# The inputs loaded ahead of the modulation slabs and squared as they lie, and the first norm and first two panels taken by rows 0 to 3, then 4 to 7

## What is computed

```python
def rmsnorm(x, w):
    xf = x.astype(jnp.float32)
    y = xf * lax.rsqrt(jnp.mean(xf * xf, axis=-1, keepdims=True) + EPS)
    return (y * w.astype(jnp.float32)).astype(x.dtype)
...
    silu_c = jax.nn.silu(c)
    silu_cc = jax.nn.silu(c_ctx)[None]
    for i in range(DEPTH):
        mod_l = jnp.split((silu_c @ ada_w[i] + ada_b[i])[:, None], 6, axis=-1)
        mod_c = jnp.split((silu_cc @ ada_w[i] + ada_b[i])[:, None], 6, axis=-1)
        h_lat = rmsnorm(x_lat, norm_w[i, 0]) * (1 + sc_l) + sh_l
        h_ctx = rmsnorm(x_ctx, norm_w[i, 0]) * (1 + sc_c) + sh_c
        ...
        # hgrn2_mixer: q, zf, zb, v, g = split(h @ w_in, ...)
```

## Time and profile before

| | |
|---|---|
| median of three runs | 2220.25 us (2220.06, 2220.25, 2223.41) |
| the profiled execution, its own time | 2224.3 us |
| its span in the profile | 2222.4 us |
| mean granted TensorE clock | 0.977 of full speed |
| PE busy over the span | 2111.2 us, 95% |
| DVE, ACT, POOL busy | 1091.4, 824.9, 49.1 us |
| read from and written to DRAM | 189.47 MB and 13.63 MB |

### The profile page before, as it was taken

One profiled execution on the slowest core, in us unless ns is written; L12 is line 12 of the kernel. 1 busy time (PEld: TensorE's weight loads), 2 busy tenths in 40 slices (PEclk: granted clock), 3 DMA queues, 4 the chain that ended last, 5 costly groups with the idle time before them and its releaser, 6 DMA issues.

```text
span 2222.4 us, 33823 instructions
## 1 busy us (share of the span) xinstructions
PE 2111.2 (95%) x13397; PEld 1882.9 (85%) x13412; DVE 1091.4 (49%) x1607; ACT 824.9 (37%) x1278; POOL 49.1 (2%) x79
## 2 busy tenths in 40 slices
PE   5899999998989999999999889999998898999998
PEld 3799989998889999999999877787875687888887
DVE  4755555567352222222223686777777544333333
ACT  2543343345132221112221543838383425532222
POOL 1000000000000000000000100000001000000000
PEclk8999999999989999999999999999999999999999
DMA  7322222223314332233322211121215132333331
GB/s 273 128 77 77 86 86 75 69 86 100 119 48 142 113 98 66 73 114 114 118 69 58 83 54 45 48 85 47 85 47 203 56 92 78 100 101 89 95 111 68
DMA packets 297512, 204.42 MB, mean 92 GB/s; under 512 B 5012, under 2 KB 289037, under 8 KB 295629
## 3 DMA queue, kind: packets, MB, share of 16 engines
q1 hardware_dynamic: 293965, 180.03, 26.7%
q0 software_dynamic: 3456, 23.09, 2.8%
HBM read 189.47 MB, written 13.63 MB: 91 GB/s over the span
## 4 chain that ended last, share of the span: by engine, by line
PE 79%; DVE 10%; ACT 6%; issue 3%; DMA 1%; SPq 0%; ACTq 0%; DVEq 0%; POOL 0%
PE G L309 66%; PE G L415 2%; PE S L765 1%; PE S L1492 1%; DVE acc L1523 1%; ACT whi L292 1%; ACT e L1367 1%; DVE hlo L646 1%; PE S L736 1%; PE S L1488 1%; DVE wlo L296 1%; DVE hn L638 1%; PE S L1688 1%; DVE cum L985 1%; PE G L421 1%
## 5 line engine op out<-in xcount | busy, mean ns | idle before, releaser
L309 PE MATMUL G<-hhi,whi 128*128 128x384 f32 (+2 forms) x2336 | 726.8, 369 | 31.7 <-DVE hlo L646 20.5
L309 PE MATMUL G<-hhi,wlo 128*128 128x384 f32 (+2 forms) x2336 | 680.8, 349 | 0.0
L309 PE MATMUL G<-hlo,whi 128*128 128x384 f32 (+2 forms) x2336 | 680.5, 349 | 0.0
L296 DVE TENSOR_TENSOR wlo<-raw,whi 128x1024 fp32r<-128x1024 f32 (+1 forms) x225 | 288.4, 1282 | 779.5 <-ACT whi L292 779.2
L292 ACT ACTIVATE whi<-raw 128x1024 fp32r<-128x1024 f32 (+1 forms) x225 | 248.7, 1106 | 941.0 <-PE G L309 470.5
L309 PEld LDWEIGHTS G<-hhi,whi 128*128 128x128 f32 x2336 | 422.7, 191 | 98.0 <-issue 35.1
L309 PEld LDWEIGHTS G<-hhi,wlo 128*128 128x128 f32 x2336 | 432.9, 190 | 20.4
L309 PEld LDWEIGHTS G<-hlo,whi 128*128 128x128 f32 x2336 | 432.8, 190 | 17.9
L309 PE MATMUL G<-mhi,whi 128*128 128x384 f32 (+2 forms) x550 | 165.6, 346 | 0.0
L309 PE MATMUL G<-mlo,whi 128*128 128x384 f32 (+2 forms) x550 | 165.2, 345 | 0.0
L309 PE MATMUL G<-mhi,wlo 128*128 128x384 f32 (+2 forms) x550 | 165.2, 345 | 0.0
(11 more groups left out here) (283 smaller groups left out, 2098.3 us busy)
## 6 DMA issues: line engine op xcount, KB each, us to landing
raw<-in_ffn_w_in_dram SPq DMA_DIRECT2D x88, 512.0 KB, 3.7
raw<-in_ffn_w_out_dram SPq DMA_DIRECT2D x32, 704.0 KB, 4.5
raw<-in_ssm_w_in_dram SPq DMA_DIRECT2D x41, 512.0 KB, 3.8
raw<-in_hg_w_in_dram SPq DMA_DIRECT2D x40, 512.0 KB, 3.8
adaw<-in_ada_w_dram SPq DMA_DIRECT2D x20, 1024.0 KB, 5.8
adaf<-in_ada_w_dram SPq DMA_DIRECT2D x20, 1024.0 KB, 4.9
ada<-in_ada_w_dram SPq DMA_DIRECT2D x4, 2048.0 KB, 13.3
raw<-in_ssm_w_out_dram SPq DMA_DIRECT2D x16, 512.0 KB, 3.9
```

The costliest lines, as they stand in the source:

```text
L296: dve.tensor_tensor(wlo[pn.slot][:, 0:kt, :], raw[pn.slot][:, 0:kt, :], f32(whi[pn.slot][:, 0:kt, :]), ALU.subtract).then_inc(s["lo"], 1)
L309: ins = pe.matmul(G[:, tl.slot, g0:g0 + n], w[pn.slot][:, k, :], r[:, k_base + k, t0:t0 + n], start=(first and k == 0 and i == 0), stop=(l ...
```

## The change

It has four parts. (1) SP: the six inputs are issued ahead of all slabs, each on its own semaphore; then slab 2 and slab 0, the panels 0 and 1, slab 3 and slab 1 (`SLABS`). The first two slabs get tiles of their own, laid over `hhi` and `hlo`, so no slab waits for a tile. Slab 2 and 0 hold the scale and shift of rows 0 to 3, slab 3 and 1 those of rows 4 to 7. (2) The squares: ACT squares each input block as it lies, with the tokens on the partitions (`sqx`, 128 x 1024), and DVE sums a block with one `tensor_reduce` into `xsum`; the sums over channels on PE are gone, and all six blocks get one mean, one power on POOL, and one spread. (3) The transposes come ahead of the slabs on PE, and the first two slabs' `strips` and `turned` behind them. (4) `norm_place` makes the first norm go by rows 0 to 3 (half 0, then half 1), then rows 4 to 7; `product_first` replaces `product_pair` in the same order, with the other two slabs' `strips` after units 2 and 4 and their `turned` after units 5 and 7; ACT copies their rows to `arow` ahead of units 5 and 7 (`first_rows`), DVE adds them into `mods` ahead of units 7 and 8 and makes the second half of `afac` (`first_mods`). The `adaw` rows come with the last unit. The copy of `x0` to DRAM now waits for unit 9 of the norm as well, and the five small operations on `lbt` and `lb` stand behind the norm on DVE.

```diff
@@ squares, norm @@
+        def norm_place(N, v):
+            return (v // KT, v % KT) if N else (v % KT // 4, v // KT * 4 + v % 4)
@@ slabs @@
+        SLABS = (2, 0, 3, 1)
+        ada, arow = (m["adahi"], m["adalo"], m["ada0"], m["ada1"]), (m["arow0"], m["arow1"])
+        def slab_strips(pe, i):
+            pe.wait_ge(s[f"slab{i}"], 16)
+            strips(pe, [(S[:, i % 2, :], ada[i])]).then_inc(s["ada"], 1)
+        def product_first(pe, pn):
+            product_begin(pe, pn, pn)
+            for u in range(2 * KT + LAG):
+                if u < 2 * KT:
+                    e, k = norm_place(0, u)
+                    pe.wait_ge(s["hlo"], u + 1)
+                    ins = product_block(pe, pn, pn, m["hhi"], m["hlo"], k, KT, SEGS, half=e, apart=False)
+                if u == 2 * KT - 1:
+                    product_end(pe, pn, ins, rows=0)
+                if u == LAG:
+                    product_begin(pe, pn + 1, pn + 1)
+                if u >= LAG:
+                    e, k = norm_place(0, u - LAG)
+                    ins = product_block(pe, pn + 1, pn + 1, m["hhi"], m["hlo"], k, KT, SEGS, half=e, apart=False)
+                if u == 2:
+                    slab_strips(pe, 2)
+                if u == 4:
+                    slab_strips(pe, 3)
+                if u == 5:
+                    pe.wait_ge(s["arows"], 1)
+                    slab_turned_of(pe, 2)
+                if u == 7:
+                    pe.wait_ge(s["arows"], 2)
+                    slab_turned_of(pe, 3)
+            product_end(pe, pn + 1, ins, turn=m["mrow0"])
+        def first_rows(act, v):
+            if v in (5, 7):
+                i = (v - 5) // 2
+                act.wait_ge(s["ada"], 5 + i)
+                act.activation(arow[i][:, :], S[:, i, :], ACT.Copy).then_inc(s["arows"], 1)
+        def first_mods(dve, v):
+            if v in (7, 8):
+                dve.wait_ge(s["ada"], v)
+                slab_mods(dve, v - 5)
+            if v == 8:
+                dve.wait_ge(s["modev"], 6)
+                factors(dve, 0, 0, 4, KT)
@@ POOL @@
-            for e in (0, 1):
-                rsqrt_half(pool, 0, e, SEGS)
+            rsqrt_pool(pool, 0, NBLK)
             pool.wait_ge(s["x"], NBLK * 2)
+            pool.wait_ge(s["hn"], KT + 1)
             pool.dma_start(x_park0, m["x0"][:, :, :]).then_inc(s["parked0"], 16)
@@ ACT @@
+            for b in range(NBLK):
+                act.wait_ge(s[f"xin{b}"], 16)
+                if b >= 2:
+                    act.wait_ge(s["sqd"], b - 1)
+                act.activation(m[f"sqx{b % 2}"][:, :], m["xin"][:, b, :], ACT.Square).then_inc(s["sq"], 1)
@@ DVE @@
+            for b in range(NBLK):
+                for q in (0, 1):
+                    u = 2 * b + q
+                    dve.wait_ge(s["xt"], u + 1)
+                    dve.tensor_copy(m["x0"][:, 4 * q:4 * q + 4, b * P:(b + 1) * P],
+                                    Gq[:, u % 4, :].rearrange("p (j t) -> p j t", j=4)).then_inc(s["x"], 1)
+                dve.wait_ge(s["sq"], b + 1)
+                dve.tensor_reduce(m["xsum"][:, b:b + 1], m[f"sqx{b % 2}"][:, :], axis=mybir.AxisListType.X,
+                                  op=ALU.add).then_inc(s["sqd"], 1)
```

More of the change, by code:

```diff
@@ L162, in memory @@
                ("colD", (P, 2, 3, HEADS)),
-               ("lbt", (P, 2, HEADS)), ("lbe", (P, 2, 3, HEADS))) <= N
+               ("lbt", (P, 2, HEADS)), ("lbe", (P, 2, 3, HEADS)),
+               ("sqx0", (P, D)), ("sqx1", (P, D)), ("xsum", (P, 8))) <= N
+    for w in ("hi", "lo"):
+        run(m_at["h" + w], (f"ada{w}", (P, KT, 512)))
     run(R, ("og", (P, HEADS, T)),
@@ L176, in memory @@
                ("act0", (P, T)), ("mid0", (P, T)), ("mrow1", (P, SLAB)), ("adaf", (P, KT, SLAB))) <= N
-    run(m_at["xin"], *[(f"{n}a{i}", (P, T)) for n in ("sq", "hn") for i in (0, 1)])
+    run(m_at["xin"], *[(f"hna{i}", (P, T)) for i in (0, 1)])
     run(m_at["mlo"], ("sqb0", (P, T)), ("sqb1", (P, T)), ("sumb", (P, T)))
@@ L790, in hg_tensor @@
             if h is None:
-                product_pair(pe, 0, pn, pn, SEGS, rows=0, turn=m["mrow0"])
+                product_first(pe, pn)
             for j in range(3 if h is None else 0, 5):
@@ new lines, in slab_turned_of, with slab_mods @@
+        def slab_turned_of(pe, i):
+            for b in range(4):
+                ins = turned(pe, slab_columns(i)[:, 2 * b:2 * b + 2], block(arow[i % 2][:, :], b))
+            ins.then_inc(s["ada"], 1)
+        def slab_mods(dve, i):
+            t = SLABS[i] * 4
+            bias = m["colB"][:, t:t + 4].rearrange("p (t a) -> p t a", a=1)
+            dve.tensor_tensor(m["mods"][:, 0, t:t + 4, :], slab_columns(i).rearrange("p (t a) -> p t a", a=2),
+                              bias.to_broadcast([P, 4, 2]), ALU.add).then_inc(s["modev"], 1)
@@ L1924, in _ @@
                 sp.dma_start(to[r0:r0 + src.shape[0], :], src).then_inc(s["rows"], 16)
-            for n in (0, 1):
-                slab_sync(sp, n)
             for b in range(NBLK):
@@ L1929, in _ @@
                 b0 = b if b < LBLK else b - LBLK
-                sp.dma_start(m["xin"][:, b, :], src[b0 * P:(b0 + 1) * P, :]).then_inc(s["xin"], 16)
-            for n in (2, 3):
-                slab_sync(sp, n)
+                sp.dma_start(m["xin"][:, b, :], src[b0 * P:(b0 + 1) * P, :]).then_inc(s[f"xin{b}"], 16)
+            for i in (0, 1):
+                slab_sync(sp, i)
+            for j, kind in ((0, QUERY), (1, FWD)):
+                load_panel(sp, At(j), cols_of(hg_w_in[0], HG_OFF[kind]), KT)
+            for i in (2, 3):
+                slab_sync(sp, i)
             def hg_loads(pn, kinds, hn_, v, vlot, h, hl):
                 for j, kind in enumerate(kinds):
-                    if kind is not None:
+                    first = isinstance(hn_, int) and hn_ == 0 and j <= 2
+                    if kind is not None and not first:
                         head = hn_ if kind != GATE else (hl if j == 0 else h)
```

124 lines of the change are left out of this document (64 added, 60 removed).

## The result

| | before | changed |
|---|---|---|
| median | 2223.89 us (7 runs, 2220.06 to 2225.92) | 2212.63 us (7 runs, 2207.65 to 2219.68) |
| ratio | | 0.995, 95% interval 0.9939 to 0.9961 |
| profiled execution, its span | 2224.3, 2222.4 us | 2219.68, 2218.0 us |
| mean granted clock there | 0.977 | 0.974 |

The change made the kernel faster by 0.5%: 11.3 us between the medians. Run twice more, each time beside the kernel before, the same kernel gave 0.9938 (0.9925 to 0.9951) and 0.9946 (0.9933 to 0.9959). The median of before had been 2220.25 over three runs when the prediction was made and came out at 2223.89 over seven.

What follows compares the result with a forecast made beforehand. PE was taken to bound most of the span, the start being a line of waits. Norm start 20.7 us earlier, 8.4 given back: 12.3 less, 2220.25 - 12.3 = 2208.0 us; range 2203 to 2212, chance 0.84.

Steps and rivals of the forecast that it cites:

- Part 2: From norm start to first panel's end: 31.0 us against 22.6, so 8.4 lost to slab work inside the norm.
- Part 1: Transfers, squares, transposes and first two slabs ahead of the norm: the norm starts 20.7 us earlier.
- t0: The time at which the norm can start on DVE; forecast 34.0 us, against 54.72 before.
- B: PE's clock after the wait for slab 0: half at first, back some four microseconds into dense work; norm starts at 34.0.
- C: PE's clock after the wait for slab 0: half throughout the work ahead of the norm, which starts at 35.4.
- the rival of a slow reduce: DVE's reduce of 1024 columns takes 2.6 us, twice an add's unit price; t0 39.8, total about 2213.8; chance 0.03.
- What was costed at nothing: Behind the norm: `lbt` operations (1.1 us) and memsets hidden by `whi`; x0's copy to DRAM hidden with 2.8 us cover.
- Stalls hidden: Rival: DVE's waits for PE at units 7 and 8 cost half or less; total 2200.6 to 2204.3; chance 0.08.
- Clock at half all through: Rival: PE's clock stays at half through the norm, first panel ends 12.3 us later, 2228.7 with one further panel; chance 0.04.

Runs made afterwards that it cites:

- the early version: Changed kernel with strips of slab 3 ahead of unit 0, of slab 1 behind unit 2, turns and adds into mods moved too: median 2204.45 us, ratio 0.9913.
- the expectation above: Written for a second run of the changed kernel with all four slabs worked off ahead of the norm, halves in old order: median 2217.05 us, ratio 0.9966.

## Why the prediction was off

The change went the way that was forecast, by the mechanism that was forecast, and by nearly the size: 12.3 us predicted, 11.3 between the medians (13.3 and 11.7 in the two repeats). That the size came so near is in part luck, as Part 2 below shows: up to the split the profiles have 8.1 to 10.3. The median landed at 2212.63, outside the range of 2203 to 2212.

- **The step that failed: "I put the median at 2220.25 - 12.3 = 2208.0".** The median of three runs stood 3.6 us under that of seven on the same kernel, and 4 us below the profiled execution, as the text said. I took the low base as given and made no room for it in the range. With 2223.89 as the base the sum is 2211.6, a microsecond from the result and just inside the range. The range held the rivals' prices and not the scatter of single runs, which reached from 2220.06 to 2225.92 for the kernel before and from 2207.65 to 2219.68 for the changed one.
- **Part 1, t0.** Transposes at 8.6 (8.57 measured), a block every 2.4 us (2.32), six done at 24.4 (24.0), strips of slab 2 at 20.1 (20.48), of slab 0 at 25.2 (25.51): right. Of the three clock cases the two repeats were B up to t0 (34.07 and 33.85 against 34.0), the first profile C (35.85 against 35.4). The reduce took 1.21 us with 1.12 to the next start, inside the bounds of 1.15 to 1.24; the rival of a slow reduce did not come about. The Trainium skill, "VectorE: DVE Perf Modes", Rules for kernel authors, calls tensor_reduce the slowest DVE operation and says to consider restructuring. It gives no factor, so the "twice" of that rival was the prediction's own. At 1.21 us for 1024 columns, beside 1.23 for the `wlo` subtract of the same width, the measurement gives no reason to restructure here.
- **Part 2, the norm.** DVE's wait ahead of unit 7: 4.0 predicted, 4.03, 4.04 and 4.04 measured. From unit 8 to the split 12.85 predicted (31.0 less 18.15), 12.9 measured, with the `adaw` rows on the path at 1.03. But unit 8 started 20.3 to 20.5 us after unit 0, not 18.15. The term mis-sized is PE's speed there. Case B took the clock as back before t0 and full from then on. In the two repeats it did come back, at 29.6 and 28.8, but fell again at 33.0 and 32.2, just ahead of t0; in the first profile it never came back before t0. The norm began at half clock in all three and had it until 41.8, 39.8 and 42.5; in the first two it fell again ahead of unit 8, at 52.0 and 50.0. The trace of before had a sign of this that the prediction did not read. It went by the return at 29, but the clock was down a second time:

```profile
45.00:46.00 1.00, 0.81 (x4) 0.50 0.00 0
...
55.00:56.00 1.00, 0.96 (x5) 0.50 1.34 522
56.00:57.00 1.00, 0.22 (x1) 0.78 1.11 472
```

  PE took up work there at 45.19, and the clock was back only at 56.4. The chain of the third profile shows what it cost:

```profile
39.50 3.31 PE S L418 x16
...
48.16 0.80 PE S L424 x8
...
50.51 2.38 PE G L312 x12
52.89 0.80 PE S L424 x8
```

  The first strips inside the norm start 5.65 us after t0 in each profile, where the prediction had 4.85. In the third they then took 3.31 instead of the 1.83 of a run at full clock, and DVE's wait ahead of unit 8 was the predicted 2.3. In the first they took 1.97, but the pieces ahead of unit 8 took 3.54 and 1.20 instead of 2.38 and 0.80, and the wait was 3.86. Each way that is 2.3 to 2.5 us, against the 2.1 to 2.3 by which unit 8 was late. So the norm grew by 10.7, not 8.4, and panel 2 was split 8.1, 10.0 and 10.3 earlier, not 12.3. The medians still moved by 11.3, 13.3 and 11.7. No profile places the difference of 1 to 3 us; before was profiled once, so its 77.34 may itself lie off its mean, and the cause stays open.
- **What was costed at nothing.** The copy to DRAM was asked for at 57.56 and landed 11.0 us later, at 68.6; DVE asked at about 69.9. Hidden, with 1.3 us of cover left. The `lbt` operations and memsets ended at 69.9, before `whi` of panel 2 was done at 70.3: hidden.
- **The rivals.** Stalls hidden: no, 4.0 and 2.3 to 3.9 were there; the early version shows how they can be. Clock at half all through: no, but it came down inside the norm, which was the rival's ground; I had put it at nothing or all.

## What to carry to other kernels

Starting a stage early is worth only what the engine that feeds it is not given to do in the meantime: the norm started 19 to 21 us earlier and gave half of it back, mostly because two runs of strips stood on PE ahead of matmuls for which DVE was waiting, and for some 2 us because PE did that work at half clock. When work is put into a stream, put it where that engine waits anyway, ahead of its first need, and ask for its result as late as it is used: the same instructions in other places won 6 us more. A predicted absolute time needs the scatter of the base in its range; three runs of the kernel before do not give it.

## What the runs showed of the hardware

The scatter between profiled executions goes with TensorE's clock. The time that an execution took behind the split, where all kernels do the same, stands here against the time at half clock from the split to the end of its span (twice the missing share of the granted clock): 76.9 to 77.0 us at half clock went with 2142.8 to 2143.8 us (four profiles), 80.3 to 87.0 with 2143.2 to 2147.0 (six), 90.7 with 2150.4, and 100.8 with 2154.7. That is about half a microsecond lost for each at half clock, and a reach of 12 us, as large as the whole effect of the change. (The 95.5, 85.3 and 71.8 of the expectation above count the same up to 2200 us only.) The clock also fell while PE was busy: at 52.0 and 58.8 in the changed kernel, in the first of the matmuls behind pauses of 1.6 and 2.4 us that had begun at full clock, and at 32.2 in its third profile, in the spread, where PE had been at work since 25.96 with a pause of 0.3 us. Filling the pause ahead of slab 0, in the two kernels with the strips done twice, took away the low stretch that began in it or just behind it, and not the next one.
